# Three small experts in place of two, some of their weights multiplied as stored, and one rounding moved ahead

## The chip, the cores and the metric

The kernel runs on one core of a Trainium2 chip. The metric is device time in microseconds (us) of one execution, as the median of several runs.

## The reference, cut to what matters

Two residual layers on 256 tokens of width 1024 (float32). Each has token mixers (attention, gated linear attention, pooling) and then a channel mixer: a dense SwiGLU in the first layer, eight experts in the second, of which each token takes two.

```python
def moe_ffn(h, w_router, w_e_gate, w_e_up, w_e_down):
    logits = jnp.einsum('bsd,de->bse', h, w_router)
    top_vals, top_idx = lax.top_k(logits, TOP_K)          # 2 of 8
    top_w = jax.nn.softmax(top_vals, axis=-1)
    combine = jnp.sum(jax.nn.one_hot(top_idx, N_EXPERTS) * top_w[..., None], axis=-2)
    y = jnp.zeros_like(h)
    for e in range(N_EXPERTS):
        y = y + combine[..., e:e + 1] * swiglu(h, w_e_gate[e], w_e_up[e], w_e_down[e])
    return y
def swiglu(h, w_gate, w_up, w_down):
    return (jax.nn.silu(h @ w_gate) * (h @ w_up)) @ w_down  # 1024 -> 1408 -> 1024
```

Only the expert part is touched by the change. On the reference's inputs the router gives the eight experts 54, 71, 64, 61, 71, 75, 55 and 61 tokens.

## The kernel before, in words

Each engine's program is written out by hand; semaphores join them. Nothing schedules but the order of the code.

**Places.** Experts 0 and 1 are run first, at places 0 and 1. The others are sorted by their number of tokens. The smallest go to the places in `SMALL` (3 and 6), the rest to the other places. A large place has room for 96 tokens (`CAP`), a small one for 64 (`FEW`). If more tokens came than there is room for, a second pass over all experts would run.

**Arithmetic.** A float32 product is made of rounded parts (type fp32r). A weight half `w` is rounded to `w_hi` by ScalarE (`round_hi`, L566), and VectorE takes the rest, `w_lo = w - w_hi` (`rest_lo`, L579). A large expert needs three matmuls for each tile (`three`, L1462 to L1464): hi by hi, lo by hi, hi by lo of tokens and weights, with 96 token columns as the stationary operand. A small expert has hi and lo of its 64 tokens side by side as 128 columns, so two matmuls do (`two`, L1467 and L1468). Its rows are then folded: ScalarE copies the result (`fold`, L2162) and one more matmul adds the lower half to the upper (L1446).

**Pieces.** An expert's weights are cut into 24 pieces (`EPIECES`): gate and up in column groups 0, 1, 2, then the down weights, in the order G0 U0 G1 U1 G2 D0 U2 D1 D2 D3. Groups 0 and 1 have three pieces each for G and U, with 3, 3 and 2 tiles of 128x512; so pieces 0 to 2 are G0, 3 to 5 U0, 6 to 8 G1, 9 to 11 U1. G2 and U2 have two pieces of four 128x384 tiles. D0 to D3 have two pieces each and are loaded with one DMA each.

**The ring.** SyncE loads pieces in order into a ring of four slots with two halves each (`ring`), so up to eight pieces are in flight or in work (`expert_loads`, L778). A load waits until the piece eight before it has been subtracted (`wait_lo`). The rounded parts have four buffers, used in turn (`w_hi`, `w_lo`, `w_hi_last`, `w_lo_last`); a rounding waits until TensorE has used the piece four before it (`split_used`). TensorE waits for `lo_ready`.

**Gathers.** Tokens are gathered by matmuls with selection matrices, in three batches (`BATCHES`). The second batch (places 2 to 4) is gathered during place 1, the third (places 5 to 7) during place 4 (`BATCH_IN`).

**Rows out.** ScalarE and VectorE scale the result (`rows_out`, L2147 and L2878) and GpSimd scatters it with an adding indirect DMA (L1735), once for a large expert and twice for a small one (upper and lower half).

**The start of the experts.** ScalarE and VectorE prepare pieces 0 to 3 of expert 0 (`EARLY` = 4) before the router's last steps: root, an Exp table load, the exponential, a Silu table load (L2213 to L2218). From piece 4 on, they work in `expert`.

## Time and profile before

| | us |
|---|---|
| median of 3 runs | 1056.73 (1056.29 to 1057.15) |
| profiled execution | 1055.96 |
| its span | 1053.9 |
| TensorE busy | 1025.3 |
| VectorE busy | 837.4 |
| ScalarE busy | 680.3 |

The span goes from the first to the last instruction; the profiled execution's own time has 2.06 us around it. Busy times are unions of what an engine's records cover. Matmuls overlap, so a busy TensorE may still have small gaps. PE is TensorE's matmul, PEld its weight load, DVE VectorE, ACT ScalarE, POOL GpSimd, SP SyncE.

### The profile page before, as it was taken

The page shows a single profiled execution, that of the slowest core. Times are in us where ns is not written, and L with a number is a line of the kernel's source. Part 1 is how long each engine was busy: PE and PEld are TensorE (multiplying, and loading weights), DVE is VectorE, ACT ScalarE, POOL GpSimd, SP SyncE. Part 2 cuts the span into 40 slices and gives each one's busy share as a digit, 9 for nine tenths or more (in the row PEclk, how much of TensorE's full clock was granted, in tenths as well). Part 3 has the DMA queues.
Part 4 walks back from the last instruction along what each step waited for, and adds up shares of the span by engine and source line. Part 5 has one row for each costly group of instructions (what it writes and reads, how often), then busy time and mean ns, then how long its engine had stood idle before and what let it go on. Part 6 is the DMA issues. An engine that isn't in the chain of part 4 may idle for free.

```text
span 1053.9 us, 15307 instructions
## 1 busy us (share of the span) xinstructions
PE 1025.3 (97%) x5557; PEld 835.6 (79%) x5557; DVE 837.4 (79%) x1213; ACT 680.3 (65%) x1013; POOL 143.9 (14%) x220
## 2 busy tenths in 40 slices
PE   8999999999999999999999999999999899999897
PEld 7988788888888888999887878777877667776675
DVE  6879776988666766687967797898889898888985
ACT  7776746556443534676665555866778787778884
POOL 5004332001100000000614000080020010101011
PEclk9999999999999999999999999999999999999999
DMA  9553544467456546363444548799899999999994
GB/s 282 194 168 111 172 130 158 162 230 270 149 209 229 171 140 190 106 222 119 130 162 146 173 141 291 267 333 332 316 331 395 381 384 389 342 396 376 391 376 141
DMA packets 131383, 253.03 MB, mean 240 GB/s; under 512 B 6638, under 2 KB 56900, under 8 KB 131300
## 3 DMA queue, kind: packets, MB, share of 16 engines
q1 hardware_dynamic: 129444, 245.93, 66.7%
q0 software_dynamic: 1392, 4.46, 2.0%
q10 hardware_dynamic: 464, 1.58, 0.4%
q8 instruction: 47, 0.77, 0.3%
q14 instruction: 36, 0.29, 0.1%
HBM read 247.49 MB, written 4.46 MB: 239 GB/s over the span
## 4 chain that ended last, share of the span: by engine, by line
PE 83%; DVE 9%; ACT 3%; issue 2%; DMA 2%; POOL 0%; SPq 0%; ACTq 0%; DVEq 0%; POOLq 0%
PE PS L904 28%; PE PS L1309 8%; PE PS L1462 7%; PE PS L1464 7%; PE PS L1463 7%; PE PS L1310 4%; PE PS L1467 2%; PE PS L1258 2%; PE PS L1257 2%; PE PS L1256 2%; DVE w_lo L579 2%; DVE w_lo_last L579 2%; PE PS L1468 2%; PE PS L928 2%; DVE m_lo L2382 2%
## 5 line engine op out<-in xcount | busy, mean ns | idle before, releaser
L579 DVE TENSOR_TENSOR w_lo<-ring,w_hi 128x1536 fp32r<-128x1536 f32 (+1 forms) x190 | 303.6, 1616 | 78.2 <-ACT w_hi L566 77.2
L566 ACT ACTIVATE w_hi<-ring 128x1536 fp32r<-128x1536 f32 (+1 forms) x191 | 258.7, 1368 | 95.4 <-PE PS L1310 47.8
L1789 ACT ACTIVATE m_hi<-ring 128x512 fp32r<-128x512 f32 (+2 forms) x256 | 157.6, 631 | 119.6 <-PE PS L904 118.1
L2382 DVE TENSOR_TENSOR m_lo<-ring,m_hi 128x512 fp32r<-128x512 f32 (+2 forms) x256 | 182.3, 743 | 58.5 <-ACT m_hi L1789 56.3
L904 PE MATMUL PS<-m_hi,h_both 128*128 128x512 f32 (+3 forms) x640 | 178.6, 365 | 0.7 <-DVE m_lo L2382 0.6
L904 PEld LDWEIGHTS PS<-m_hi,h_both 128*128 128x128 f32 x640 | 113.0, 188 | 19.8 <-DVE m_lo L2382 2.5
L1309 PE MATMUL PS<-h_both,w_hi 128*128 128x512 f32 x352 | 124.4, 398 | 0.0
L904 PE MATMUL PS<-m_lo,h_both 128*128 128x512 f32 (+3 forms) x320 | 115.0, 359 | 0.0
L1310 PE MATMUL PS<-h_both,w_lo 128*128 128x256 f32 x352 | 98.6, 280 | 0.0
L1462 PE MATMUL PS<-w_hi,hTe 128*96 128x512 f32 (+1 forms) x240 | 90.2, 376 | 1.6 <-DVE w_lo L579 1.6
L1464 PE MATMUL PS<-w_lo,hTe 128*96 128x512 f32 (+1 forms) x240 | 89.7, 374 | 0.0
L1463 PE MATMUL PS<-w_hi,hTe 128*96 128x512 f32 (+1 forms) x240 | 89.1, 371 | 0.0
L579 DVE TENSOR_TENSOR w_lo_last<-ring,w_hi_last 128x1536 fp32r<-128x1536 f32 (+1 forms) x47 | 78.1, 1663 | 8.9 <-ACT w_hi_last L566 8.4
L1309 PEld LDWEIGHTS PS<-h_both,w_hi 128*128 128x128 f32 x352 | 66.1, 188 | 15.9
L566 ACT ACTIVATE w_hi_last<-ring 128x1536 fp32r<-128x1536 f32 (+1 forms) x47 | 66.3, 1410 | 6.7 <-PE PS L1464 6.7
L904 PEld LDWEIGHTS PS<-m_lo,h_both 128*128 128x128 f32 x320 | 60.2, 188 | 9.1
L1310 PEld LDWEIGHTS PS<-h_both,w_lo 128*128 128x128 f32 x352 | 66.4, 189 | 0.2
L1735 POOL DMA_INDIRECT out_dram<-ye,row_of x9 | 21.1, 2344 | 284.0 <-DVE ye L2878 124.8
L1462 PEld LDWEIGHTS PS<-w_hi,hTe 128*96 128x96 f32 x240 | 38.8, 162 | 13.2 <-issue 2.8
L1464 PEld LDWEIGHTS PS<-w_lo,hTe 128*96 128x96 f32 x240 | 38.8, 162 | 11.4
L1463 PEld LDWEIGHTS PS<-w_hi,hTe 128*96 128x96 f32 x240 | 38.9, 162 | 10.7 <-issue 0.2
L1632 POOL TENSOR_TENSOR big<-big,rnb 128x256 f32<-128x256 f32 x22 | 17.2, 811 | 220.4 <-DVE big L2780 220.4
(438 smaller groups left out, 2054.2 us busy)
## 6 DMA issues: line engine op xcount, KB each, us to landing
ring<-in_w_in_dram SPq DMA_DIRECT2D x39, 1024.0 KB, 5.2
ring<-in_w_exp_gate_dram SPq DMA_DIRECT2D x48, 768.0 KB, 8.2
ring<-in_w_exp_up_dram SPq DMA_DIRECT2D x48, 768.0 KB, 8.6
ring<-in_w_exp_down_dram SPq DMA_DIRECT2D x24, 1536.0 KB, 9.4
ring<-in_w_branch_dram SPq DMA_DIRECT2D x12, 1024.0 KB, 5.1
ring<-in_w_ffn_gate_dram SPq DMA_DIRECT2D x12, 768.0 KB, 5.4
ring<-in_w_ffn_up_dram SPq DMA_DIRECT2D x12, 768.0 KB, 6.1
ring<-in_w_ffn_down_dram SPq DMA_DIRECT2D x6, 1536.0 KB, 6.5
```

The costliest lines, as they stand in the source:

```text
L566: act.activation(split_parts(u, j)[0], ring[:, i % NSLOT, w0:w0 + words], ACT.Copy)\
L579: dve.tensor_tensor(lo, ring[:, (j // 2) % NSLOT, w0:w0 + words], hi.bitcast(F32), SUB).then_inc(sem(f"lo_ready{b}"), 1)
L904: mm = pe.matmul(dst, l, r, start=(kt == 0 and x == 0 and y == 0), stop=(kt == total - 1 and y == 2), skip_group_check=True)
L928: mm = pe.matmul(dsts[a], xx[:, kt, t], ww[:, k, :], start=(kt == 0 and y == 0 and (a == 0 or fulls[0] is not None)), stop=(kt == total - ...
L1309: pe.matmul(both, hi[:, k, c], h_both[:, :, kt, :], start=(kt == 0), stop=False, skip_group_check=True)
L1310: mm = pe.matmul(both[:, 0, :], lo[:, k, c], h_hi[:, kt, :], start=False, stop=(kt == KD - 1), skip_group_check=True)
L1462: pe.matmul(dst, xhi, whi, start=start, stop=False)
L1463: pe.matmul(dst, xlo, whi, start=False, stop=False)
L1464: return pe.matmul(dst, xhi, wlo, start=False, stop=stop)
L1735: pool.indirect_dma_start(out.rearrange("b t d -> (b t) d"), bass.IndirectOffsetOnAxis(row_of[0:slots_of(e), e:e + 1], 0), ye[some, e % 2, ...
L1789: act.activation(hi, raw, ACT.Copy).then_inc(sem("m_hi_ready"), 1)
L2382: dve.tensor_tensor(lo, raw, hi.bitcast(F32), SUB).then_inc(sem("m_lo_ready"), 1)
```

## The change

Places 2, 4 and 6 are small, and the third batch of tokens is gathered during place 3. Pieces 1, 4, 7 and 10 of a small expert are neither rounded nor subtracted: TensorE waits for the load itself and multiplies the piece in the ring as float32, once for each tile, with the 128 token columns read as float32. Its matmuls raise the two semaphores that rounding and subtraction would have raised. The load eight pieces later waits for TensorE's use of such a piece instead of its subtraction. And expert 0's piece 4 is rounded before the tables and subtracted between two small steps of the router.

```diff
-SMALL = (3, 6)
+SMALL = (2, 4, 6)
+WHOLE = (1, 4, 7, 10)
+def as_stored(n, e, j):
+    return isinstance(n, int) and e in SMALL and j in WHOLE
-BATCH_IN = {1: 1, 4: 2}
+BATCH_IN = {1: 1, 3: 2}
-EARLY, EARLY_PAIRS = 4, 3
+EARLY, EARLY_PAIRS = 5, 3
...
             def expert_loads(wg, wu, wd, x, uo, e, again=False):
                     if of >= 2 * NSLOT:
-                        wait_lo(sp, (1, uo), of - 2 * NSLOT)
+                        for gone in range(j - 2 * NSLOT, of - 2 * NSLOT + 1):
+                            if as_stored(uo, e, gone):
+                                wait_used(sp, (1, uo), gone)
+                            elif gone == of - 2 * NSLOT or as_stored(uo, e, gone + 1):
+                                wait_lo(sp, (1, uo), gone)
...
+                        if as_stored(n, e, j):
+                            wait_landed(pe, j, 1, n)
+                            b, _ = half_buffer(expert_unit(n), j)
+                            words, w0 = half_words(1, j)
+                            stored = ring[:, j // 2 % NSLOT, w0:w0 + words].rearrange("p (k c) -> p k c", k=nk)
                         for k in range(nk):
                             kt = k0 + k
+                            if as_stored(n, e, j):
+                                mm = pe.matmul(PS[:, 2 * (g % 2) + up, 0:gn * P], hTe_few[:, kt, :, :].bitcast(F32), stored[:, k, :],
+                                               start=kt == 0, stop=False)
+                                if k < nk - 1:
+                                    mm.then_inc(sem((f"hi_ready{b}", f"lo_ready{b}")[k]), 1)
+                                continue
...
-                    if j < HALVES and not (j < EARLY and isinstance(n, int) and n == 0):
+                    if j < HALVES and not as_stored(n, e, j) and not (j < EARLY and isinstance(n, int) and n == 0):
                         round_hi(act, expert_unit(n), j, 1, n, e == NE - 1 and EPIECES[j][0] == EORDER[-1])
...
-                    for j in range(NSPLIT, EARLY):
+                    round_hi(act, expert_unit(0), NSPLIT, 1, 0)
+                    squared(2 * DEPTH - 1, 1), roots(2 * DEPTH - 1)
+                    for j in range(NSPLIT + 1, EARLY):
                         round_hi(act, expert_unit(0), j, 1, 0)
-                    squared(2 * DEPTH - 1, 1), roots(2 * DEPTH - 1)
...
                 dve.tensor_tensor(rsm[:, 0:2], rsm[:, 0:2], inv_rms(2 * DEPTH - 1), MUL).then_inc(sem("routing_known"), 1)
+                for j in range(ESPLIT, EARLY):
+                    rest_lo(dve, (1, 0), j)
                 dve.wait_ge(sem("rsp_ready"), 1)
```

SyncE's queue at place 2, pieces 9 to 16 of the expert (`up` and `gate` loads, then D0 and a U2 piece), before:

```order
L778 DMA ring<-in_w_exp_up_dram 128x3x512 [waits lo_ready1]
L778 DMA ring<-in_w_exp_up_dram 128x3x512 [waits lo_ready2]
L778 DMA ring<-in_w_exp_up_dram 128x2x512 [waits lo_ready3]
L778 ISA [waits lo_ready0]
L778 DMA ring<-in_w_exp_gate_dram 128x4x384
L778 ISA [waits lo_ready1]
L778 DMA ring<-in_w_exp_gate_dram 128x4x384
L778 DMA ring<-in_w_exp_down_dram 128x3x1024 [waits lo_ready3]
L778 DMA ring<-in_w_exp_up_dram 128x4x384 [waits lo_ready0]
```

and the same place after:

```order
L794 DMA ring<-in_w_exp_up_dram 128x3x512 [waits split_used1]
L794 DMA ring<-in_w_exp_up_dram 128x3x512 [waits lo_ready2]
L794 DMA ring<-in_w_exp_up_dram 128x2x512 [waits lo_ready3]
L794 ISA [waits split_used0]
L794 DMA ring<-in_w_exp_gate_dram 128x4x384
L794 ISA [waits lo_ready1]
L794 DMA ring<-in_w_exp_gate_dram 128x4x384
L794 DMA ring<-in_w_exp_down_dram 128x3x1024 [waits split_used3,lo_ready2]
L794 DMA ring<-in_w_exp_up_dram 128x4x384 [waits lo_ready0]
```

The loads that follow pieces 1, 4 and 7 now wait for TensorE (`split_used`); the order of the loads is the same.

ScalarE at the start of expert 0 (its piece 3 goes to `w_hi_last`, piece 4 to `w_hi`), before:

```order
L566 ACTIVATE w_hi_last<-ring 128x1536
L1813 ACTIVATE big,small<-x_tok 128x1024
L1818 ACTIVATE rns<-small,eps 128x2
L2213 ACT_TABLE_LOAD
L2213 ACTIVATE rsm<-eps 128x1
L2215 ACTIVATE rsp<-rns 128x2
L2217 ACTIVATE rsm<-rsm 128x2
L2218 ACT_TABLE_LOAD
L2218 ACTIVATE small<-eps 128x1
L566 ACTIVATE w_hi<-ring 128x1536
L566 ACTIVATE w_hi<-ring 128x1024
```

and after:

```order
L578 ACTIVATE w_hi_last<-ring 128x1536
L1840 ACTIVATE big,small<-x_tok 128x1024
L1845 ACTIVATE rns<-small,eps 128x2
L578 ACTIVATE w_hi<-ring 128x1536
L2241 ACT_TABLE_LOAD
L2241 ACTIVATE rsm<-eps 128x1
L2243 ACTIVATE rsp<-rns 128x2
L2245 ACTIVATE rsm<-rsm 128x2
L2246 ACT_TABLE_LOAD
L2246 ACTIVATE small<-eps 128x1
L578 ACTIVATE w_hi<-ring 128x1024
```

Piece 4's rounding has moved past both table loads and the four small steps between and behind them.

## Rows read from the trace of the kernel before

**Rows 1.** The page's throughput line, the span in 40 equal slices.
```profile
GB/s 282 194 168 111 172 130 158 162 230 270 149 209 229 171 140 190 106 222 119 130 162 146 173 141 291 267 333 332 316 331 395 381 384 389 342 396 376 391 376 141
```
**Rows 2.** ScalarE's timeline, output rows (L2147); columns: start, length, engine, line, what, [idle before].
```profile
766.41 0.69 ACT L2147 ACTIVATE ye<-PS,rw 96x512 f32<-96x512 f32 x1 [0.96 <-PE PS L1464]
...
813.35 0.69 ACT L2147 ACTIVATE ye<-PS,rw 96x512 f32<-96x512 f32 x1 [1.02 <-PE PS L1464]
...
857.42 0.69 ACT L2147 ACTIVATE ye<-PS,rw 128x512 f32<-128x512 f32 x1 [0.91 <-PE PS L1468]
...
909.61 0.69 ACT L2147 ACTIVATE ye<-PS,rw 96x512 f32<-96x512 f32 x1 [1.02 <-PE PS L1464]
...
956.50 0.69 ACT L2147 ACTIVATE ye<-PS,rw 96x512 f32<-96x512 f32 x1 [1.02 <-PE PS L1464]
...
999.88 0.69 ACT L2147 ACTIVATE ye<-PS,rw 128x512 f32<-128x512 f32 x1 [0.91 <-PE PS L1468]
...
1044.96 0.69 ACT L2147 ACTIVATE ye<-PS,rw 96x512 f32<-96x512 f32 x1 [3.16 <-PE PS L1464]
```
**Rows 3.** Windows: stretch, length, busy PE, PEld, DVE, ACT, POOL; clock, DMA share, GB/s.
```profile
814.00:857.00 43.00, 36.13 (x162) 26.86 (x160) 38.55 (x31) 34.80 (x36) 2.70 (x1) 1.00 1.05 385
858.00:909.00 51.00, 50.52 (x251) 38.45 (x250) 45.09 (x56) 39.88 (x58) 3.30 (x2) 1.00 1.04 378
```
**Rows 4.** The throughput line of 800 to 870 us, in 40 slices.
```profile
GB/s 403 386 389 387 387 386 387 386 391 379 390 385 330 249 402 391 383 409 400 380 371 400 410 405 410 412 407 391 389 385 390 382 390 385 386 389 364 283 407 403
```
**Rows 5.** ScalarE's timeline: roundings of D0's first piece that a landing released.
```profile
788.89 1.49 ACT L566 ACTIVATE w_hi<-ring 128x1536 fp32r<-128x1536 f32 x1 [1.93 <-DMA ring<-in_w_exp_down_dram]
...
835.40 1.49 ACT L566 ACTIVATE w_hi<-ring 128x1536 fp32r<-128x1536 f32 x1 [1.47 <-DMA ring<-in_w_exp_down_dram]
...
881.67 1.49 ACT L566 ACTIVATE w_hi<-ring 128x1536 fp32r<-128x1536 f32 x1 [0.55 <-DMA ring<-in_w_exp_down_dram]
...
1022.62 1.49 ACT L566 ACTIVATE w_hi<-ring 128x1536 fp32r<-128x1536 f32 x1 [1.95 <-DMA ring<-in_w_exp_down_dram]
```
**Rows 6.** Waits of SyncE's queue, 700 to 1050 us: total, times, longest.
```profile
SPq L778 <- DVE w_lo L579: 141.0, 95, 4.8
```
**Rows 7.** TensorE's timeline: float32 calls in attention, rounded matmuls of an expert.
```profile
90.58 0.60 PE L1072 MATMUL PS<-qk 96*128 96x256 f32 x2
91.01 0.38 PE L1071 MATMUL PS<-qk 96*128 96x128 f32 x2
...
905.18 0.40 PE L1462 MATMUL PS<-w_hi,hdT_hi 128*96 128x512 f32 x1
905.41 0.40 PE L1463 MATMUL PS<-w_hi,hdT_lo 128*96 128x512 f32 x1
```
**Rows 8.** Groups by line, 640 to 1054 us: count, busy, mean ns, idle before.
```profile
L579 DVE TENSOR_TENSOR w_lo<-ring,w_hi 128x1536 fp32r<-128x1536 f32 x102 | 177.6, 1754 | 25.0 <-ACT w_hi L566 24.2
L566 ACT ACTIVATE w_hi<-ring 128x1536 fp32r<-128x1536 f32 x103 | 151.7, 1484 | 19.6 <-DMA ring<-in_w_exp_down_dram 10.0 <-PE PS L1464 8.1 <-DMA ring<-in_w_exp_up_dram 0.7
```
**Rows 9.** SyncE's timeline: loads of pieces 9 to 11 at place 2.
```profile
767.43 3.83 SPq L778 DMA_DIRECT2D ring<-in_w_exp_up_dram  x3
```
**Rows 10.** Windows, the start of place 2.
```profile
764.00:776.00 12.00, 12.00 (x54) 8.34 (x53) 11.69 (x10) 8.66 (x7) 3.02 (x1) 1.00 0.95 283
```
**Rows 11.** GpSimd's timeline: the scatter of place 0's rows.
```profile
765.86 3.02 POOL L1735 DMA_INDIRECT out_dram<-ye,row_of  x1 [58.26 <-issue]
```
**Rows 12.** The page's queues: packets, MB, share of 16 engines' span.
```profile
q0 software_dynamic: 1392, 4.46, 2.0%
```
**Rows 13.** Timelines of ScalarE, VectorE and TensorE at the start of expert 0.
```profile
666.00 3.79 ACT L566 ACTIVATE w_hi<-ring 128x1536 fp32r<-128x1536 f32 x3
...
667.50 4.56 DVE L579 TENSOR_TENSOR w_lo<-ring,w_hi 128x1536 fp32r<-128x1536 f32 x3 [2.82 <-ACT w_hi L566]
...
669.41 0.44 PE L1462 MATMUL PS<-w_hi,hTe 128*96 128x512 f32 x1 [1.00 <-DVE w_lo L579]
...
687.16 0.39 PE L1462 MATMUL PS<-w_hi,hTe 128*96 128x384 f32 x1 [0.60 <-DVE w_lo L579]
```

More of the change, by code:

```diff
@@ L551, in in_columns, with wait_landed @@
             return x.rearrange("p (k c) -> p k c", k=EDOWN[-1][1])
+        def wait_landed(eng, j, kind, n):
+            i = j // 2
+            half, per, place = half_place(kind, j)
+            dense_per = half_place(0, next(x for x in range(HALVES) if x // 2 % NSLOT == i % NSLOT and half_place(0, x)[0] == half))[1]
+            eng.wait_ge(sem(f"half_full{i % NSLOT}{half}"), 16 * (per * n + dense_per * NDENSE * kind + place + 1))
         def round_hi(act, u, j, kind, n, columns=False):
@@ L556, in round_hi @@
             i = j // 2
-            half, per, place = half_place(kind, j)
-            dense_per = half_place(0, next(x for x in range(HALVES) if x // 2 % NSLOT == i % NSLOT and half_place(0, x)[0] == half))[1]
-            act.wait_ge(sem(f"half_full{i % NSLOT}{half}"), 16 * (per * n + dense_per * NDENSE * kind + place + 1))
+            wait_landed(act, j, kind, n)
             if not isinstance(uses, int) or uses > 1:
@@ L750, in unit_loads, with expert_loads @@
                             sp.dma_start(dst.rearrange("p (k c) -> p k c", k=KD // 2), src).then_inc(sem(f"half_full{s}{half}"), 16)
-            def expert_loads(wg, wu, wd, x, uo, again=False):
+            def expert_loads(wg, wu, wd, x, uo, e, again=False):
                 wg, wu, wd = wg[x], wu[x], wd[x]
@@ L810, in _ @@
             eg, eu, ed = A["w_exp_gate"][0], A["w_exp_up"][0], A["w_exp_down"][0]
-            expert_loads(eg, eu, ed, 0, 0)
+            expert_loads(eg, eu, ed, 0, 0, 0)
             for e in range(1, FIXED):
-                expert_loads(eg, eu, ed, e, e)
+                expert_loads(eg, eu, ed, e, e, e)
             def expert_in(e):
@@ L819, in _ @@
             for e in range(FIXED, NE):
-                expert_loads(eg, eu, ed, expert_in(e), e)
+                expert_loads(eg, eu, ed, expert_in(e), e, e)
             sp.wait_ge(sem("routing_known"), ROUTING_KNOWN["passes_known"])
@@ L826, in _ @@
                     for e in range(NE):
-                        expert_loads(eg, eu, ed, expert_in(e) if e >= FIXED else e, r * NE + e, again=True)
+                        expert_loads(eg, eu, ed, expert_in(e) if e >= FIXED else e, r * NE + e, e, again=True)
         @block.tensor
@@ L1495, in expert @@
                     last = e == NE - 1 and name == EORDER[-1]
-                    if not last:
+                    if not last and not as_stored(n, e, j):
                         hi, lo = parts(expert_unit(n), j)
@@ L2940, in expert @@
                             tokens(r, BATCH_IN[e], g)
-                    if j < HALVES and not (j < EARLY and isinstance(n, int) and n == 0):
+                    if j < HALVES and not as_stored(n, e, j) and not (j < EARLY and isinstance(n, int) and n == 0):
                         rest_lo(dve, expert_unit(n), j, e == NE - 1 and EPIECES[j][0] == EORDER[-1])
@@ L3024, in one_pass @@
                 if isinstance(r, int):
-                    for j in range(2, EARLY):
+                    for j in range(2, ESPLIT):
                         rest_lo(dve, (1, 0), j)
```

## The prediction

> **What bounds the kernel now.** I read the throughput line over the whole span first. From the 27th to the 39th slice (685 to 1028 us) the queues move 316 to 396 GB/s, and this is where experts run [rows 1]. The view of rows leaving the experts dates them: the output rows of places 1 to 7 start at 766.41, 813.35, 857.42, 909.61, 956.50, 999.88 and 1044.96 us [rows 2]. So a small expert takes 44.07 us (place 3) or 43.38 us (place 6), a large one 46.94 or 46.89 us (places 2 and 5), and a large one that also gathers the tokens of the last batch 52.19 us (place 4).
>
> Which engine sets these? The windows say that TensorE has hardly a gap in the large expert at place 4 (50.52 of 51 us), while it is busy for only 36.13 of 43 us in the small one at place 3. VectorE is at 38.55 of 43 there, and the DMA column reads 1.05 [rows 3]. The finer throughput line from 800 to 870 us shows a plateau: 371 to 412 GB/s in 36 of its 40 slices, with two dips down to 249 and 283 [rows 4]. A plateau with the queues never empty is a limit of the queues. The rounding engine confirms it. Its starts that were released by a landing load of the down weights stand at 788.89 (place 2), 835.40 (place 3), 881.67 (place 4) and 1022.62 us (place 7) [rows 5]. These are the same piece of consecutive experts, so the loads need 46.51, 46.27 and then 140.95 / 3 = 46.98 us an expert. That is the key number: **the loads need 46.3 us an expert, which is more than a small expert's 43.4 and nearly a large one's 46.9.** A small expert only eats up the lead of the loads that a large one has left. And the loads wait for room: SyncE waits 141 us on the subtraction of half loads (first of two such rows) between 700 and 1050 us [rows 6].
>
> So there are two tables to keep: engines, 46.9 + 44.1 + 52.2 + 46.9 + 43.4 + 45.1 = 278.6 us for places 2 to 7, and loads, 6 x 46.3 = 277.8 us. They are balanced; taking work off the engines alone cannot give what it removes.
>
> **The change part by part.**
>
> *A third small expert.* Before, places 2 to 7 are large, small, large with gathers, large, small, large; afterwards small, large with gathers, small, large, small, large. It is one large expert fewer. By the engines this saves 46.9 - 43.7 = 3.2 us. Its rows fit: the reference's router gives experts 2 to 7 of its inputs 64, 61, 71, 75, 55 and 61 tokens, and the three smallest (55, 61, 61) are at most 64, so no second pass runs.
>
> *Half loads as stored.* Pieces 1, 4, 7 and 10 of a small expert have three 128x512 tiles each, so 12 matmuls in float32 replace 24. Two rounded ones follow each other at 0.23 us [rows 7]. The trace has float32 calls of 128 and 256 columns, in attention, each shown as two records: the two records of a 256-column call take from 90.58 to 91.01 us, 0.43 us [rows 7]. None has 512 columns. The bounds for one are 0.46 us (it costs what the pair costs) and 0.86 us (twice the 0.43); as the cost per column is what the rows show, I take 0.86. TensorE then has 12 x (0.86 - 0.46) = 4.8 us more work in each small expert, 36.1 + 4.8 = 40.9 us, still below 46.3. So it costs nothing, as long as the loads are the cover. ScalarE loses 4 x 1.484 and VectorE 4 x 1.754 = 7.0 us in each small expert [rows 8]. Neither is late last where the loads bound, so I book no gain.
>
> *The ring.* What is new is a wait: a piece's place in the ring, which the subtraction used to free, is freed by TensorE's last matmul on it. SyncE issues in order, so everything behind a held piece waits too. At place 2 TensorE starts at about 766.2 (place 1's rows leave at 766.41); piece 0 needs 6 x 0.23 = 1.4 us and piece 1 3 x 0.86 = 2.6, so piece 1 is let go at about 770.2, and the load behind it, issued at 767.43 before [rows 9], goes out 2.8 us later. The ones behind pieces 4 and 7 are about 2.6 and 2.8 us late in the same way. If the queues hold other loads meanwhile, this is hidden. They don't quite at that place: from 764 to 776 us they move 283 GB/s against the plateau's 387 [rows 10, 4], 12 x (1 - 283/387) = 3.2 us lost, part of it to the scatter of place 0's rows issued at 765.86 [rows 11]. Afterwards the hole comes in one piece and the scatter falls into it; then the loads run without a gap, as the faster small expert never lets them run out of room. Bounds for this place: 3.2 us gained (no loss at all) and 2.8 us lost (the hole comes on top). I take 0.7 gained, near the middle, as the same bytes pass in the same time.
>
> *Places 4 to 7.* From 881.67 to 1022.62 us the loads need 140.95 us where three experts at 46.3 would need 138.9: 2.05 us are lost, and this happens where large follows large (places 4 to 5, then 6) and the ring is full. After the change large and small alternate, so it happens once, at the start of place 4. I take half, 1.0 us gained; bounds 2.05 gained and 2.8 lost (one held piece not hidden).
>
> *One more scatter.* The third small expert writes 64 rows twice in place of 96 rows once. The scatter queue takes 2.0% of the 1053.9 us, 21.1 us for 4.46 MB [rows 12], 4.7 us a MB; 32 rows of 4 KB more are 0.13 MB, 0.6 us on the loads' path. The wider tables of the third expert (one more comparison per token half in place 1) lie beside its matmuls.
>
> *The fifth rounding.* Expert 0's piece 4 is rounded at 666.00 us, after two table loads; VectorE takes its rest at 667.50, and TensorE, idle for 1.00 us, starts it at 669.41 [rows 13]. Afterwards ScalarE does it before the tables, at about 662.9, and VectorE ends its rest at about 666.2; the 1.00 us goes. What is late next is piece 5: ScalarE's work is only put in another order, so that its rounding still ends at about 666.00 + 1.4 + 1.0 = 668.4. VectorE could start its rest then, where it now does at about 667.50 + 1.7 = 669.2; it is full from there to TensorE's next wait, before 687.16 [rows 13], and so ahead by 0.8 us at most. I take 0.5; bounds 0 and 1.0. The row scales, for which TensorE reads a value that now comes after this rounding, are needed at 667.54 and would be there at 666.4.
>
> *Sum:* -0.7 - 1.0 + 0.6 - 0.5 = **-1.6 us**. The profiled execution took 1055.96 us with a span of 1053.9; the median of the runs is 0.77 higher, and the sum goes onto it: 1056.73 - 1.6 = **1055.1 us**.
>
> **A rule against this reading.** The plateau measured here is 371 to 412 GB/s. The Trainium skill, "DMA: Bandwidth & Descriptors", Specifications, gives 435 GB/s as the fabric's ceiling and about 358 GB/s as HBM's limit per core. The trace is above the second, so that one does not bind here, and no run here shows the first reached. By the ceiling, as an estimate from the page, an expert's 17.3 MB (3 x 1408 x 1024 x 4 bytes) would need 39.8 us and the loads would not bound a small expert; this is the first rival below, whose price is worked out from rows alone.
>
> **The rivals.**
>
> *The engines bound, not the loads* (0.14). Then each small expert runs at its 40.9 us of TensorE: 3 x 40.9 + 52.2 + 46.9 + 45.1 = 266.9 in place of 278.6, and up to 11.7 us go. For it: VectorE is at 38.55 of 43 us [rows 3] and gives up 7.0. Against it: the plateau and the landings that release ScalarE [rows 4, 5]. With the loads never waiting for room the bounds above add up to 3.2 + 2.05 + 1.0 - 0.6 = 5.7 us, so its time is about 1051, and 1045 at the very best.
>
> *The held ring starves the queues* (0.17, slower). Place: the start of each small expert, where TensorE comes late from a large one. Price: 2.8 us for each held chain that is not hidden. It decides where fewer than two half loads are in flight when the held piece is let go. With two of the three hit, the gains of both places gone: 1056.73 + 2 x 2.8 + 0.6 - 0.5 = 1062.4; with one, 1059.6. For it: the 283 GB/s at place 2 [rows 10]. Against it: at the plateau several loads are queued.
>
> *The freed time is absorbed* (0.08): the two places give nothing, and 1056.73 + 0.6 - 0.5 = 1056.8 is left.
>
> *The float32 call costs twice what I take* (0.01): 1.72 us, 51.2 us a small expert, 4.9 over the loads each, some 1070.
>
> **How the numbers follow.** The forecast has 0.60; its own range is 1052.6 to 1057.2. This kernel's measurement cannot tell less than 0.2%, 2.1 us, from no change. Of the forecast's 0.60 I put 0.22 below 1054.6 and 0.38 within. Faster: 0.22 + 0.14 = 0.36. Same: 0.38 + 0.08 = 0.46. Slower: 0.17 + 0.01 = 0.18. The range from 1050.5 (most of the engines' case) to 1060 (one chain not hidden) leaves out two in ten.
>
> **What would show it.** Right: the landings that release ScalarE stay 46 to 47 us apart, TensorE is idle for some 5 us in each small expert, the throughput from place 3 on stays at the plateau, and the wait before expert 0's piece 4 is gone. Wrong: small experts of 41 us with landings that close up (first rival), or slices below 300 GB/s at the start of places 2, 4 and 6 with SyncE waiting on TensorE (second). A float32 call of 512 columns far from 0.86 us would upset the sum for TensorE.

## The result and the profile after

The changed kernel takes 1058.42 us (median of 11 runs, 1056.54 to 1062.45); the kernel before, on the same chip, took 1056.29 (11 runs, 1054.14 to 1057.15). The ratio is 1.0028, 95% interval 1.0017 to 1.0040, so the change costs about 3.0 us where 1.6 us were to be gained. Below, "against before" is always (ratio - 1) x 1056 us. Two single runs that took far longer (1129.2 us of the kernel before, 2012.9 us of e4 below) are left out of the ratios.

The profiled execution of the changed kernel took 1062.45 us (span 1060.6). It is the slowest of its 11 runs, and part of that is nothing the change did. One window, from 645 to 660 us, which still lies ahead of the first expert matmul, of the kernel after and then of the kernel before (columns as in [rows 3]):

```profile
645.00:660.00 15.00, 14.76 (x80) 11.74 (x78) 9.69 (x25) 6.30 (x9) 1.36 (x2) 0.77 0.98 339
```

```profile
645.00:660.00 15.00, 14.49 (x103) 11.98 (x102) 12.46 (x30) 8.40 (x13) 1.36 (x2) 1.00 0.96 346
```

The granted clock of TensorE is 0.77 on the mean of these 15 us, against 1.00: of its two levels, 2.4 and 1.2 GHz, it had the lower for 6.9 us. Expert 0 begins 3.0 us later for that (piece 4 is rounded at 665.58 us here, and at 662.61 in run e1 below, which has the same order up to there). So I compare stretches that begin and end inside the experts, and windows that begin at the same event of each kernel.

The throughput line after, in answer to [rows 1]:

```profile
GB/s 287 196 156 126 164 133 147 185 230 268 153 178 236 159 155 190 110 199 159 91 193 127 178 159 267 279 335 328 308 324 391 382 312 395 380 390 375 394 377 134
```

The 33rd slice (848 to 875 us), with the end of place 3 and the start of place 4, reads 312 where it read 384; the 35th, around the end of place 4, reads 380 where it read 342. A loss has moved from the end of place 4 to its start, and grown. ScalarE's roundings that a landing of D0 released, places 2 to 7 (in answer to [rows 5]):

```profile
792.35 1.49 ACT L578 ACTIVATE w_hi<-ring 128x1536 fp32r<-128x1536 f32 x1 [1.30 <-DMA ring<-in_w_exp_down_dram]
...
839.86 1.49 ACT L578 ACTIVATE w_hi<-ring 128x1536 fp32r<-128x1536 f32 x1 [1.71 <-DMA ring<-in_w_exp_down_dram]
...
889.94 1.48 ACT L578 ACTIVATE w_hi<-ring 128x1536 fp32r<-128x1536 f32 x1 [0.38 <-DMA ring<-in_w_exp_down_dram]
...
936.24 1.49 ACT L578 ACTIVATE w_hi<-ring 128x1536 fp32r<-128x1536 f32 x1 [2.39 <-DMA ring<-in_w_exp_down_dram]
...
982.55 1.48 ACT L578 ACTIVATE w_hi<-ring 128x1536 fp32r<-128x1536 f32 x1 [0.75 <-DMA ring<-in_w_exp_down_dram]
...
1029.68 1.49 ACT L578 ACTIVATE w_hi<-ring 128x1536 fp32r<-128x1536 f32 x1 [2.36 <-DMA ring<-in_w_exp_down_dram]
```

From place to place this is 47.51, 50.08, 46.30, 46.31 and 47.13 us; [rows 5] had 46.51 and 46.27 for the first two. From place 2 to place 7 it is 237.33 us against 233.73, 3.6 us more. This one number per profile, the **D0 stretch**, is used below. It leaves out what happens before place 2 and the first part of place 2 too, in which pieces 1, 4, 7 and 10 are multiplied. So the table has a second stretch, **rows 1 to 7**: from the first output row of place 1 to that of place 7 (before, by [rows 2], 1044.96 - 766.41 = 278.55 us). It holds all three small places.

The windows at the starts of places 2 and 4, in answer to [rows 10]:

```profile
764.00:776.00 12.00, 12.00 (x47) 7.95 (x46) 7.97 (x12) 6.46 (x9) 2.49 (x2) 1.00 0.93 248
868.00:880.00 12.00, 12.00 (x41) 7.48 (x40) 7.78 (x8) 7.80 (x8) 1.44 (x1) 1.00 0.88 268
```

Both are below 300 GB/s, with TensorE busy all the time. (The first lies 2.6 us earlier in its place than [rows 10]; moved by that, it reads 270 GB/s, against 283.) And SyncE's queue now waits for TensorE's float32 matmuls (L1549; a wait stands at the load's line or at the wait's own), in answer to [rows 6]:

```profile
SPq L794 <- DVE w_lo L591: 118.8, 77, 4.8
...
SPq L794 <- PE PS L1549: 26.0, 9, 5.1
...
SPq L537 <- PE PS L1549: 12.3, 3, 4.3
```

These are the signs that the prediction had named for its second rival.

### The profile page after: what moved, and what is told of

It reads as the page before. It is cut to its first block, busy times and chain, and to the rows that moved or that the text cites. A ratio compares the mean times of both kernels' runs of the same rounds, so it can differ in the third digit from the quotient of the medians.

```text
span 1060.6 us, 15166 instructions
## 1 busy us (share of the span) xinstructions
PE 1029.1 (97%) x5501; PEld 831.9 (78%) x5501; DVE 817.8 (77%) x1204; ACT 663.3 (63%) x1005; POOL 142.1 (13%) x221
## 4 chain that ended last, share of the span: by engine, by line
PE 80%; DVE 10%; DMA 5%; ACT 3%; issue 2%; POOL 0%; SPq 0%; DVEq 0%; ACTq 0%; POOLq 0%
PE PS L920 27%; PE PS L1325 8%; PE PS L1478 5%; PE PS L1480 5%; PE PS L1479 5%; PE PS L1326 4%; DMA ring<-in_w_exp_down_dram 3%; PE PS L1549 3%; DVE w_lo L591 3%; PE PS L1483 2%; PE PS L1484 2%; PE PS L1272 2%; PE PS L1274 2%; PE PS L1273 2%; DVE w_lo_last L591 2%
## 5 line engine op out<-in xcount | busy, mean ns | idle before, releaser
L591 DVE TENSOR_TENSOR w_lo<-ring,w_hi 128x1536 fp32r<-128x1536 f32 (+1 forms) x181 | 289.4, 1610 | 94.4 <-ACT w_hi L578 92.9
L578 ACT ACTIVATE w_hi<-ring 128x1536 fp32r<-128x1536 f32 (+1 forms) x182 | 245.5, 1361 | 101.5 <-PE PS L1326 47.8
L591 DVE TENSOR_TENSOR w_lo_last<-ring,w_hi_last 128x1536 fp32r<-128x1536 f32 (+1 forms) x44 | 72.8, 1656 | 10.3 <-ACT w_hi_last L578 9.8
L1478 PE MATMUL PS<-w_hi,hTe 128*96 128x512 f32 (+1 forms) x200 | 75.6, 378 | 1.2 <-DVE w_lo L591 1.0
L1480 PE MATMUL PS<-w_lo,hTe 128*96 128x512 f32 (+1 forms) x200 | 74.9, 374 | 0.0
L1479 PE MATMUL PS<-w_hi,hTe 128*96 128x512 f32 (+1 forms) x200 | 74.5, 372 | 0.0
L578 ACT ACTIVATE w_hi_last<-ring 128x1536 fp32r<-128x1536 f32 (+1 forms) x44 | 61.8, 1404 | 6.7 <-PE PS L1480 5.0
L1762 POOL DMA_INDIRECT out_dram<-ye,row_of x10 | 18.4, 1841 | 287.6 <-ACT ye L2176 124.7
L920 PE MATMUL PS<-h_both,m_hi 128*128 128x256 f32 x256 | 47.0, 285 | 0.0
L1483 PE MATMUL PS<-w_hi,hTs 128*128 128x384 f32 (+1 forms) x93 | 37.3, 401 | 5.4 <-DVE w_lo L591 5.4
L1478 PEld LDWEIGHTS PS<-w_hi,hTe 128*96 128x96 f32 x200 | 32.4, 162 | 11.6 <-issue 3.1
```

What stands on the lines that cost most here:

```text
L578: act.activation(split_parts(u, j)[0], ring[:, i % NSLOT, w0:w0 + words], ACT.Copy)\
L591: dve.tensor_tensor(lo, ring[:, (j // 2) % NSLOT, w0:w0 + words], hi.bitcast(F32), SUB).then_inc(sem(f"lo_ready{b}"), 1)
L920: mm = pe.matmul(dst, l, r, start=(kt == 0 and x == 0 and y == 0), stop=(kt == total - 1 and y == 2), skip_group_check=True)
L1478: pe.matmul(dst, xhi, whi, start=start, stop=False)
L1479: pe.matmul(dst, xlo, whi, start=False, stop=False)
L1480: return pe.matmul(dst, xhi, wlo, start=False, stop=stop)
```

## The experiments

Theories at the start: the **held ring** (pieces multiplied as stored keep their ring places until TensorE is done, the loads behind start late), against **the third small expert** itself, **TensorE's float32 time**, and **the fifth rounding**. Each kernel was timed beside the kernel before on the same chip; a difference of two runs of the table is uncertain by about 1.4 us.

| run | against before, us | 95% interval | D0 stretch, us | rows 1 to 7, us |
|---|---|---|---|---|
| before | 0 | | 233.73 | 278.55 |
| after | +3.0 | +1.8 to +4.2 | 237.33 | 282.46 |
| e1 fifth rounding only | -1.6 | -2.5 to -0.6 | 234.11 | 278.26 |
| e2 third small expert only | +1.2 | +0.2 to +2.1 | 234.53 | 278.35 |
| e3 as stored only | +3.8 | +2.3 to +5.2 | 239.03 | 283.04 |
| e4 e1 and e2, nothing as stored | -0.4 | -1.5 to +0.6 | 234.61 | 279.08 |
| e5 e4 and the hold | +0.8 | -0.1 to +1.8 | 235.21 | 279.77 |
| e6 e4 and float32 calls | +4.6 | +3.2 to +6.1 | | 283.70 |
| e7 after, late two pieces | -0.4 | -1.4 to +0.5 | 234.23 | 278.22 |
| e8 e4, one scatter short | -1.8 | -2.7 to -0.8 | 233.75 | 277.96 |
| e9 after, two-byte calls | +1.3 | +0.1 to +2.4 | 235.36 | 281.68 |
| e10 e4, three scatters short | -3.1 | -4.1 to -1.9 | 231.42 | 275.89 |
| e11 after, early two pieces | +2.3 | +1.4 to +3.3 | 237.23 | 282.20 |
| e12 after, place 2 only | +0.2 | -0.8 to +1.3 | 235.73 | 280.98 |
| e13 after, stand-in calls | +2.9 | +1.5 to +4.2 | 234.93 | 279.99 |
| e14 e4, float32 early two | +0.5 | -0.5 to +1.7 | 236.75 | 281.21 |
| e15 e4, float32 late two | +0.6 | -0.6 to +1.9 | | 279.66 |
| e16 e5 and float32 calls | +4.8 | +3.4 to +6.1 | | 284.69 |

Both stretches are of one profiled execution each. Where the D0 stretch is empty, no landing released the rounding at place 2. The mean granted clock from rows 1 to rows 7 reads 1.00 in all but e9 (0.98) and e12 (0.99).

### One part at a time (e1 to e4)

All are the changed kernel with parts put back by their constants:

```diff
 e1: SMALL = (3, 6), BATCH_IN = {1: 1, 4: 2}, WHOLE = ()
 e2: EARLY = 4, WHOLE = ()
 e3: SMALL = (3, 6), BATCH_IN = {1: 1, 4: 2}, EARLY = 4
 e4: WHOLE = ()
```

e1. 

> The kernel before with one part of the change, expert 0's fifth piece rounded ahead of the tables; small experts stay at places 3 and 6 and nothing is multiplied as stored. Held ring (the as-stored pieces keep their ring places until TensorE is done with them, and the loads behind them start late): this part is harmless, 0 to -1.1 us against the kernel before, because the 1.00 us idle of TensorE in expert 0 goes and at most part of it is lost again. Third expert (the third small expert itself costs): the same, 0 to -1.1 us. Fifth rounding harms (it delays the tables and with them the row scales): +1 to +3 us.

Measured: -1.6 us; the fifth rounding is a gain. TensorE's first wait in expert 0 is now the one behind [rows 13]'s last row, at 686.29 (first row, e1; second, after):

```profile
686.29 0.39 PE L1478 MATMUL PS<-w_hi,hTe 128*96 128x384 f32 x1 [1.04 <-DVE w_lo L591]
```

```profile
689.28 0.39 PE L1478 MATMUL PS<-w_hi,hTe 128*96 128x384 f32 x1 [1.01 <-DVE w_lo L591]
```

It was at 687.16, so 0.87 us of the 1.00 are kept in e1. The changed kernel has the same wait (1.01 us) and is as e1 there, 3.0 us later by the clock told of above. The profile of e1 gains more later, but by the clock, which in this execution stays at 1.00 from 720 to 735 us and in the execution shown of before does not (before, then e1). The medians hold some of this too: nine of e1's eleven runs have a mean clock of 0.998 or more, and seven of the 26 of the kernel before beside them.

```profile
720.00:735.00 15.00, 15.00 (x82) 11.72 (x81) 11.60 (x24) 9.19 (x15) 0.00 (x0) 0.89 0.86 316
```

```profile
720.00:735.00 15.00, 15.00 (x90) 11.87 (x89) 12.83 (x27) 10.79 (x18) 0.00 (x0) 1.00 0.95 337
```

e2. 

> The kernel before with one part of the change, small experts at places 2, 4 and 6 instead of 3 and 6, every piece rounded, four early roundings. Held ring: -1.7 to +0.6 us against the kernel before (what the prediction took for this part: starts and ring-full losses -1.7, one more scatter +0.6), its load holes at the starts of places 2, 4 and 6 gone. Third expert: +1.5 to +3 us, since this part alone is then the loss.

Measured: +1.2 us, between the two expectations. It is near the limit of what the runs tell: from rows 1 to rows 7, the profiles have 278.35 us against 278.55. The D0 roundings of e2 (places 2, 3, 4, 7):

```profile
788.84 1.49 ACT L578 ACTIVATE w_hi<-ring 128x1536 fp32r<-128x1536 f32 x1 [0.79 <-DMA ring<-in_w_exp_down_dram]
...
835.96 1.49 ACT L578 ACTIVATE w_hi<-ring 128x1536 fp32r<-128x1536 f32 x1 [0.92 <-DMA ring<-in_w_exp_down_dram]
...
885.12 1.49 ACT L578 ACTIVATE w_hi<-ring 128x1536 fp32r<-128x1536 f32 x1 [0.65 <-DMA ring<-in_w_exp_down_dram]
...
1023.37 1.49 ACT L578 ACTIVATE w_hi<-ring 128x1536 fp32r<-128x1536 f32 x1 [2.37 <-DMA ring<-in_w_exp_down_dram]
```

Place 2 stands where it stood (788.84 for 788.89). From place 3 to 4 it takes 49.16 us in place of 46.27, and from 4 to 7 138.25 in place of 140.95. So the time lost on a full ring is not halved: it goes from places 4 to 7 to the start of place 4.

e3. 

> The kernel before with one part of the change, four pieces of each of the two small experts (places 3 and 6) multiplied as stored, four early roundings. Held ring: +2 to +5 us against the kernel before, two held chains of 1.4 to 4.6 us each less what the later experts regain, and a stretch below 300 GB/s at the start of place 3 and of place 6. Third expert: within 1 us of before.

Measured: +3.8 us. The as-stored pieces do it, without a third small expert and without the fifth rounding. The small places are 3 and 6 here, as before, and neither follows a gathering one.

e4. 

> The changed kernel with nothing multiplied as stored: small experts at places 2, 4 and 6 and five early roundings. Held ring: 2 to 4 us below the changed kernel, so 0 to 2 us below the kernel before; the load of piece 9 of place 4 is then issued when piece 1 has been rounded, as in the kernel before, and not 5 us later. Third expert or fifth rounding: within 1 us of the changed kernel, +1.5 to +2.5 us against the kernel before.

Measured: -0.4 us, 3.4 below the changed kernel. The parts add up: -1.6 + 1.2 = -0.4, and with 3.4 for the as-stored pieces +3.0. SyncE's queue at the start of place 4, pieces 6 to 8 and then 9 to 11, in e4 and in the changed kernel:

```profile
856.08 4.55 SPq L794 DMA_DIRECT2D ring<-in_w_exp_gate_dram  x3
861.80 4.32 SPq L794 DMA_DIRECT2D ring<-in_w_exp_up_dram  x3
```

```profile
862.03 4.54 SPq L794 DMA_DIRECT2D ring<-in_w_exp_gate_dram  x3
871.71 1.92 SPq L794 DMA_DIRECT2D ring<-in_w_exp_up_dram  x3
```

Piece 9 is issued 5.7 us behind piece 6 in e4 and 9.7 us in the changed kernel.

### The hold, or TensorE's time (e5, e6)

```diff
 e5: WHOLE, HELD = (), (1, 4, 7, 10)
-    if as_stored(uo, e, gone):
+    if held(uo, e, gone):
         wait_used(sp, (1, uo), gone)
 e6: WHOLE, WORDS = (), (1, 4, 7, 10)
+    if isinstance(n, int) and e in SMALL and j in WORDS:
+        mm = pe.matmul(PS[...], hTe_few[:, kt, :, :].bitcast(F32), hi[:, k, :].bitcast(F32), start=kt == 0, stop=False)
+        continue
```

e5. 

> The changed kernel with the hold alone: pieces 1, 4, 7 and 10 of places 2, 4 and 6 are rounded and multiplied in two parts as everywhere, but SyncE lets the load that takes such a piece's ring place wait until TensorE is done with the piece, as it does for a piece multiplied as stored. Held ring: +2 to +3.5 us against the kernel before, as the changed kernel (+3.0), with SyncE waiting 4 to 5 us behind TensorE at the start of place 4 and landings there 4 us or more late. Float32 time (the cost is TensorE's: 36 calls of 0.87 us against 0.46): -1 to +0.6 us against the kernel before, as without anything stored (-0.4).

Measured: +0.8 us. The waits are all there, as in the changed kernel (SyncE's queue, 700 to 1056 us):

```profile
SPq L798 <- PE PS L1488: 19.6, 6, 3.8
...
SPq L541 <- PE PS L1488: 14.2, 3, 4.8
```

33.8 us of waiting on TensorE, against 38.3 after, cost 1.3 us over e4, no more than the uncertainty (0.7 us by rows 1 to 7). My theory of the held ring as the main cause fell here.

e6. 

> The changed kernel with the float32 multiplication alone: pieces 1, 4, 7 and 10 of places 2, 4 and 6 are rounded and their ring places given back as everywhere, but TensorE multiplies them in one float32 call for each 128 rows, from the first rounded part (the second part's product is left out for these pieces). Held ring: -1 to +1 us against the kernel before; TensorE's 36 calls more of 0.41 us (14.8 us) lie beside waits for loads. Float32 time: +2 to +3.5 us, as the changed kernel.

Measured: +4.6 us, 5.1 over e4, with not one load held. So TensorE's time is not hidden. The chain of work that ended last, in shares of 30 us, by line. The 30 us hold the end of a large place and the first 23 us of the small place that follows, or nearly so: place 3 of before (806 to 836), and place 4 of e4 (855 to 885), after (861 to 891) and e6 (856 to 886). As-stored calls are L1549, in e6 L1555.

```profile
by line: PE PS L1467 18.9%; PE PS L1468 13.1%; DVE w_lo_last L579 11.8%; ACT w_hi_last L566 9.9%; PE PS L1464 8.5%; issue 8.0%; PE PS L1462 7.8%; PE PS L1463 7.7%; DVE w_lo L579 5.9%; ACT w_hi L566 5.0%; PE PS L1430 2.0%; PE PS L1446 1.6%;
```

```profile
by line: PE PS L1483 19.5%; PE PS L1484 13.6%; DVE w_lo_last L591 11.8%; ACT w_hi_last L578 9.9%; issue 8.1%; PE PS L1478 7.8%; PE PS L1480 7.7%; PE PS L1479 7.7%; DVE w_lo L591 5.9%; ACT w_hi L578 4.9%; PE PS L1446 2.0%; PE PS L1462 1.6%;
```

```profile
by line: PE PS L1549 34.3%; PE PS L1483 14.0%; PE PS L1484 13.9%; PE PS L1479 7.7%; PE PS L1480 7.7%; PE PS L1478 7.0%; DVE w_lo L591 5.9%; ACT w_hi L578 5.0%; PE PS L1446 2.0%; issue 2.0%; PE PS L1462 1.6%; ACT big L2205 0.1%; ACTq L573 0.
```

```profile
by line: PE PS L1555 35.1%; PE PS L1483 10.1%; PE PS L1484 10.0%; PE PS L1480 8.4%; PE PS L1478 7.8%; PE PS L1479 7.7%; DVE w_lo_last L591 5.9%; ACT w_hi_last L578 5.0%; ACT w_hi L578 5.0%; issue 4.3%; PE PS L1446 2.0%; PE PS L1462 1.6%; PE
```

No load is among the entries shown, not even in the kernel before: there, as in e4, the chain goes through TensorE and the rounding. So the loads were no cover in these 30 us, and the kernel before already showed it. In the changed kernel 34.3% of the chain is float32 calls, in e6 35.1%.

How much room has TensorE there? The first 12 and 44 us behind the first output row of the place before (PE busy first), for place 4 of e4 and of after:

```profile
861.86:873.86 12.00, 10.01 (x41) 7.12 (x40) 10.30 (x9) 10.82 (x11) 2.69 (x1) 1.00 1.03 333
861.86:905.86 44.00, 37.67 (x168) 27.87 (x167) 39.94 (x32) 35.68 (x36) 2.69 (x1) 1.00 1.04 376
```

```profile
867.82:879.82 12.00, 12.00 (x42) 7.48 (x41) 7.81 (x7) 7.98 (x8) 1.44 (x1) 1.00 0.88 268
867.82:911.82 44.00, 39.86 (x164) 27.91 (x163) 33.70 (x28) 31.02 (x31) 1.44 (x1) 1.00 1.00 358
```

and the first 12 us of place 3 in the kernel before and in e3:

```profile
813.35:825.35 12.00, 10.01 (x41) 7.11 (x40) 10.39 (x9) 11.03 (x12) 2.70 (x1) 1.00 1.05 359
```

```profile
811.72:823.72 12.00, 11.96 (x41) 7.42 (x40) 7.54 (x7) 8.27 (x10) 1.44 (x1) 1.00 1.05 363
```

e4 leaves TensorE 6.3 us of 44, but only 2.0 of the first 12. In the changed kernel 4.1 us are still free over the 44, and none in the first 12. In e3 the first 12 us of place 3 are as full, 11.96 us against 10.01 in the kernel before. The call itself costs what I took: six records of one piece,

```profile
868.95 2.73 PE L1549 MATMUL PS<-ring,hTs 128*128 128x512 f32 x6
```

follow each other at (2.73 - 0.59) / 5 = 0.43 us, two to a call, 0.86 us. Each as-stored piece adds 3 x 0.4 = 1.2 us, and two of them and the start of a third stand in the first 12 us, which had 2.0 to give.

### Early or late in the expert (e7, e11, e12)

```diff
 e7:  WHOLE = (7, 10)
 e11: WHOLE = (1, 4)
 e12: as_stored(...): ... e == 2 and j in WHOLE
```

e7. 

> The changed kernel with two pieces of each small expert as stored, 7 and 10, in place of four: 1 and 4 are rounded as before. Held ring: the holes behind pieces 1 and 4 go (the loads of pieces 9 and 12 are issued as in the kernel without as-stored pieces), those behind 7 and 10 stay; at places 4 and 6 ScalarE runs behind its loads up to D0, so these two still cost some of it: +0.5 to +2 us against the kernel before, between -0.4 and +3.0. Float32 time: half of the 3.4 us, +1.3 us. (This run tells the size of the early holes, not the two theories apart.)

Measured: -0.4 us, as e4: below what I expected. SyncE still waits 19.2 us for TensorE on these pieces,

```profile
SPq L537 <- PE PS L1549: 16.4, 3, 5.5
...
SPq L794 <- PE PS L1549: 2.8, 3, 0.9
```

and it costs nothing.

e11. 

> The changed kernel with the two early pieces of each small expert as stored, 1 and 4, in place of four; 7 and 10 are rounded. Float32 time at the wrong place (TensorE is behind while a small expert begins and caught up by piece 7): the whole loss stays, +2 to +3.5 us against the kernel before. If the loss goes by the count of pieces wherever they stand: +1.3 us.

Measured: +2.3 us; the early two carry 2.7 of the 3.4 us. For pieces that are held and not rounded the place decides, not the count.

e12. 

> The changed kernel with the four as-stored pieces at place 2 alone; places 4 and 6 are small experts with every piece rounded. If the loss is made where TensorE is furthest behind its loads (place 4, and place 6 after it): 0 to +0.8 us against the kernel before (-0.4 without any and about +1 for place 2, of which later experts give part back). If each place costs a third: +0.8 to +1.2 us.

Measured: +0.2 us, 0.6 over e4. The interval holds both expectations, so this run decides nothing.

### The hold without float32 time (e9, e13)

```diff
 e9:
+    for again in range(2):
+        mm = pe.matmul(PS[...], hTe_few[:, kt, :, :].bitcast(BF16)[:, :, 1::2], stored[:, k, :].bitcast(BF16)[:, 1::2], ...)
 e13:
+    for again in range(2):
+        mm = pe.matmul(PS[...], hTe_few[:, kt, :, :], hTs[:, TSLOT[e], 0:gn * P], ...)
```

e9. 

> The changed kernel, with its held ring places and without rounding for pieces 1, 4, 7 and 10 of places 2, 4 and 6, but TensorE multiplies them in two two-byte calls for each 128 rows (the upper halves of the stored words, their product taken twice) instead of one float32 call: TensorE's time for these pieces goes back to that of the two rounded parts. Float32 time (14.8 us more of TensorE where small experts begin behind their loads): -1 to +1 us against the kernel before, 2 to 4 us below the changed kernel. Held ring: still +2 to +3 us, no more than 1 us below the changed kernel. The run of the hold alone (+0.8 us) speaks for the first.

Measured: +1.3 us, 1.7 below the changed kernel and 1.7 above e4: between the two. But its clock is not that of the others (last section).

e13. 

> The changed kernel with the ring places held until TensorE is done and no rounding for pieces 1, 4, 7 and 10 of places 2, 4 and 6, but in place of the float32 call TensorE makes two calls of the rounded kind over a stand-in that lies in SBUF (the tokens' own columns; these pieces' product is left out): the two-byte run without its clock dips. If the hold is the smaller share (+1.3 us when it stood alone) and the float32 time the larger: 0 to +1 us against the kernel before. If the hold is the larger share when nothing is rounded: +1.5 to +3 us.

Measured: +2.9 us, which reads as the hold; but the mean clock of ten of its twelve runs is 0.990 to 0.995, against 0.996 to 0.999 in 21 of 23 runs of the kernel before, so the medians compare clocks too. At like clocks e13 is not above the kernel before: its six runs at 0.993 to 0.995 took 1055.96 to 1059.52 us, the six such runs of the kernel before, over all experiments, 1058.33 to 1059.78, and the changed kernel's two, at 0.993, 1061.02 and 1062.45. The profiled execution has a mean clock of 0.997. Its chain around the start of place 4 (857 to 887 us), and its windows:

```profile
by line: DMA ring<-in_w_exp_down_dram 35.5%; PE PS L1550 9.2%; PE PS L1478 7.8%; PE PS L1480 7.7%; PE PS L1483 7.7%; PE PS L1479 7.7%; PE PS L1484 6.1%; DVE w_lo_last L591 5.9%; ACT w_hi L578 5.0%; ACT w_hi_last L578 5.0%; issue 3.8%; PE PS
```

```profile
863.86:875.86 12.00, 11.28 (x49) 8.71 (x48) 9.45 (x8) 7.99 (x8) 1.44 (x1) 1.00 0.85 271
863.86:907.86 44.00, 36.08 (x165) 27.63 (x163) 34.13 (x29) 31.04 (x31) 1.44 (x1) 1.00 0.99 360
```

The chain runs through a load (35.5%), as the prediction had it, and TensorE has 7.9 of 44 us free. The loads have as deep a hole as in the changed kernel (271 GB/s, against 268), so the hole by itself is not the loss. The first output rows of places 1 and 7, of e4, e13 and after:

```profile
764.46 0.69 ACT L2174 ACTIVATE ye<-PS,rw 96x512 f32<-96x512 f32 x1 [0.96 <-PE PS L1480]
...
1043.54 0.69 ACT L2174 ACTIVATE ye<-PS,rw 96x512 f32<-96x512 f32 x1 [3.15 <-PE PS L1480]
```

```profile
766.38 0.69 ACT L2175 ACTIVATE ye<-PS,rw 96x512 f32<-96x512 f32 x1 [0.96 <-PE PS L1480]
...
1046.37 0.69 ACT L2175 ACTIVATE ye<-PS,rw 96x512 f32<-96x512 f32 x1 [3.15 <-PE PS L1480]
```

```profile
768.99 0.69 ACT L2174 ACTIVATE ye<-PS,rw 96x512 f32<-96x512 f32 x1 [0.96 <-PE PS L1480]
...
1051.45 0.69 ACT L2174 ACTIVATE ye<-PS,rw 96x512 f32<-96x512 f32 x1 [3.15 <-PE PS L1480]
```

279.08, 279.99 and 282.46 us: at this clock the hold without float32 time costs 0.9 us, and the float32 calls, the only difference between e13 and after, 2.5 us more. (The D0 stretch, without the first part of place 2, gives 0.3 and 2.4.) That is one profile each; the medians, at unlike clocks, do not show it.

### What adds to what (e14 to e16)

```diff
 e14: e6 with WORDS = (1, 4)
 e15: e6 with WORDS = (7, 10)
 e16: e5 and e6 in one, HELD = WORDS = (1, 4, 7, 10)
```

e14. 

> The kernel with the float32 multiplication alone (rounded and given back as everywhere, one float32 call from the first part), at pieces 1 and 4 of each small expert only, so 7.4 us more of TensorE instead of 14.8. If the place decides for TensorE's time too: nearly the whole of what four pieces cost, +3 to +4.6 us against the kernel before. If it goes by the count: +2 us.

Measured: +0.5 us, 1.0 over e4; neither expectation.

e15. 

> The kernel with the float32 multiplication alone (pieces rounded and given back as everywhere, one float32 call from the first part), at pieces 7 and 10 of each small expert only. Four such pieces cost 5.0 us and the early two 1.0 us over the kernel with none. If the late two make up the rest as long as they are rounded too: +3 to +4 us against the kernel before. If the four cost more only together, because TensorE then has no time left before the loads: within 1 us of before (-0.4 to +1).

Measured: +0.6 us, 1.0 over e4. The early and the late two cost about 1 us each, within the uncertainty, and all four 5.1: they are dear together, when they use up TensorE's room. The profiles agree in the main: from rows 1 to rows 7, 2.1 and 0.6 us over e4 by halves, and 4.6 together. What stays open is e11: its two early pieces, held and not rounded, cost 2.7 us where e14's cost 1.0, and the difference is little more than the uncertainty.

e16. 

> The changed kernel with all pieces rounded: hold and float32 multiplication as in the changed kernel, at pieces 1, 4, 7 and 10, but the pieces are rounded as well and the float32 call reads the first part. Against the changed kernel this tells what leaving the rounding out gives back. If hold (+1.3 us) and float32 time with rounding (+5.0 us) add up: +5.5 to +6.5 us against the kernel before, so leaving the rounding out gives back about 3 us of it. If the hold no longer matters once TensorE is late (both make the same loads late): +4.5 to +5 us. If leaving the rounding out gives nothing: +3 us, as the changed kernel.

Measured: +4.8 us, as e6 without the hold. Once TensorE is late by its own work, holding the ring places for it adds nothing that the medians show (1.0 us by the profiles' rows 1 to 7). Leaving the rounding out, all that the changed kernel has over e16, gives back 1.8 us.

### The scatter (e8, e10)

```diff
-    some = slice(half * FEW, half * FEW + slots_of(e))
+    count = 2 if half (e8: and e == 4) else slots_of(e)
+    some = slice(half * FEW, half * FEW + count)
```

e8. 

> The changed kernel with nothing as stored, and the second scatter of place 4 cut from 64 rows to 2 (62 rows of the sum are left out there), so that about as many rows are scattered as in the kernel before. If the third small expert's +1.2 us is its scatter: 1 to 1.5 us below the same kernel with the whole scatter (which stood at -0.4 us against before), so -1.4 to -1.9 us. If it is that the place 2 start and the ring-full losses gave nothing: -0.4 to -1.0 us (at most the 0.6 us that the prediction took for the scatter).

Measured: -1.8 us, 1.4 below e4.

e10. 

> The changed kernel with nothing as stored, and the second scatter of each of places 2, 4 and 6 cut from 64 rows to 2 (62 rows of the sum are left out at each). If a second scatter costs 1.3 us, as the run with one cut tells against the one with none cut: 3.9 us below the latter, -4.3 us against the kernel before. If it costs the 0.6 us that the prediction took: -2.2 us. If nothing: -0.4 us.

Measured: -3.1 us, 2.7 below e4 for three scatters, 0.9 us each. The scatter queue's rows of e4 and e10, in answer to [rows 12]:

```profile
q0 software_dynamic: 1440, 4.59, 2.1%
```

```profile
q0 software_dynamic: 1296, 3.83, 1.7%
```

0.76 MB less, 3.6 us for each MB; a second scatter of 64 rows costs 0.9 us (with an uncertainty of about 0.5).

## Why the prediction was wrong, point by point

**The step that failed** is the one on half loads as stored: TensorE "has 12 x (0.86 - 0.46) = 4.8 us more work in each small expert, 36.1 + 4.8 = 40.9 us, still below 46.3. So it costs nothing, as long as the loads are the cover." The 0.86 is right, and so nearly is the sum: TensorE is idle for 4.1 of 44 us in place 4 after, where "some 5 us in each small expert" were forecast. The cover is not there: a mean over a whole expert was set against a mean over a whole expert. At the start of a small place that follows a large one, TensorE comes late and the chain runs through it and the rounding, in the kernel before as well; the first 12 us had 2.0 us to give, and afterwards they have none, with 34.3% of the chain in float32 calls. e3 shows the same at place 3, from which the 36.13 of 43 us came [rows 3]. Measured: the as-stored pieces cost 3.4 us in place of 0 (e4 to after; 3.8 in e3). By the profiles 2.5 of it go to the float32 calls (e13 to after) and 0.9 to the hold (e4 to e13).

**The ring.** The holes came where the second rival put them, at places 2 and 4, with SyncE waiting on TensorE. The rival's sign and size (1059.6 for one chain) came true, its cause only in part: the hold by itself costs 1.3 us with an uncertainty of 1.4 (e5), and 0.2 on top of the float32 time (e16 to e6), well within the uncertainty. Without rounding it is the smaller share, 0.9 us, by one profile of e13; the medians of e9 and e13 cannot confirm it, because these kernels changed the clock as well.

**Place 2 and places 4 to 7**, -0.7 and -1.0: together about +0.3 us by the runs (e2's +1.2 less a scatter's 0.9; e4, too, stands 1.2 above e1). The profiles have less, -0.2 us for e2 against before and 0.8 for e4 against e1, from rows 1 to rows 7. The gain of 1.7 is not seen in the runs, and its size stays open. The lost time was not a sum of disturbances that get rarer, but followed the large gathering place to its new position.

**One more scatter**, +0.6: 0.9 from e10, 1.4 from e8; the sign is right and the size was somewhat low.

**The fifth rounding**, -0.5 with bounds 0 and -1.0: 0.87 us in the profile, -1.6 (-2.5 to -0.6) by the runs, which have part of it from a higher clock. Right; the 0.87 is what the profile puts down to the change.

**The engines as the bound** (first rival) did not come: with nothing as stored, the D0 landings of e4 stand 234.61 us apart from place 2 to 7, an expert still needs 46.9 us, and the third small expert saves nothing of the 3.2 us that the engines' sum gives it.

The sum by parts is -1.6 + 1.2 + 3.4 = +3.0 us. e1, the fifth rounding alone, is 1.6 us below the kernel before and 4.6 below the changed one, the best of the kernels that do the whole computation.

## What to carry to other kernels

A resource that has room on the mean over a stage has it only where the chain of waits does not run through it: read the chain of the very stretch in which the added work will stand. Here that chain could be read in the trace of the kernel before. And compare windows that begin at the same event, not at the same time. Work added to an engine can cost little in each half and much as a whole, once it takes the room that was left. And when two transfers or engines are balanced, moving a slow stage moves its loss with it.

## What the runs showed of the hardware that was not expected

Less work on TensorE went with a lower clock. In e9, where shorter calls took the place of the float32 ones and TensorE waited for loads, four windows behind the starts of places 2 and 4 read (columns as before):

```profile
780.00:784.00 4.00, 2.90 (x12) 1.46 (x12) 0.93 (x2) 1.57 (x3) 0.00 (x0) 1.00 1.04 353
784.00:788.00 4.00, 1.34 (x5) 0.88 (x6) 2.42 (x2) 3.51 (x3) 0.00 (x0) 0.77 1.02 401
880.00:884.00 4.00, 2.18 (x9) 0.99 (x7) 2.50 (x2) 2.91 (x4) 0.00 (x0) 1.00 1.05 402
884.00:888.00 4.00, 3.42 (x12) 3.21 (x13) 2.84 (x3) 1.60 (x2) 0.00 (x0) 0.65 1.04 380
```

TensorE is busy for 2.90 of 4 us and 1.34 of the next 4, in which the granted clock falls from 1.00 to 0.77 on the mean; at place 4, 2.18 of 4 us go before 0.65. (A mean between 0.5 and 1 is a mixture of the levels of 1.2 and 2.4 GHz.) e9's twelve runs have mean clocks of 0.989 to 0.997, nine of them below 0.996; the changed kernel's eleven have 0.993 to 0.998, two below 0.996. So a kernel that gives TensorE less to do can lose part of that gain to the clock, and a comparison of medians then says less about the part that was taken away.

A float32 call of 512 columns with 128 rows is shown as two records and takes 0.86 us, in proportion to the 0.43 us of 256 columns in [rows 7].
